# Expert value sums of a PEER layer: from half of each group by Strassen's scheme to all of it

## What is computed

```python
def block(args):
    xb, eb, gb = args
    act = jax.nn.gelu(jnp.einsum('td,tkd->tk', xb, u[eb]))
    return jnp.einsum('tk,tkd->td', gb * act, v[eb])
```

## Time and profile before

| | before |
|---|---|
| median of 3 runs | 1782.0 us (1780.98 to 1785.47) |
| the profiled execution, its time | 1781.31 us |
| its span, first to last instruction | 1779.5 us |
| TensorE busy | 1722.6 us, 97% |
| VectorE busy | 1460.9 us, 82% |
| ScalarE busy | 723.3 us, 41% |
| GpSimd busy | 381.7 us, 21% |

### The profile page before, as it was taken

The page is one execution under the profiler, slowest core; times in us unless marked ns, Lnnn a source line. Parts: engine busy times, 40 slices in busy tenths (PEclk is TensorE's granted clock), DMA queues, the critical chain, the costliest instruction groups (busy, mean ns, idle before and its releaser), DMA issues.

```text
span 1779.5 us, 24820 instructions
## 1 busy us (share of the span) xinstructions
PE 1722.6 (97%) x8316; PEld 1397.7 (79%) x8316; DVE 1460.9 (82%) x2495; ACT 723.3 (41%) x903; POOL 381.7 (21%) x171
## 2 busy tenths in 40 slices
PE   5999999999999999999999999999999999999997
PEld 4774688888777788878888888888888888888885
DVE  7898779999699953388888788887878888787889
ACT  2451433332389962344343343433334343343430
POOL 1000264664300014431111111111111111111102
PEclk8999999999999999999999999999999999999999
DMA  9544210245369997654444444444444444444431
GB/s 382 220 161 165 115 43 1 101 142 191 123 192 284 283 287 257 233 195 149 148 144 148 165 147 159 145 141 150 149 169 147 149 146 147 154 147 166 150 122 70
DMA packets 137358, 293.07 MB, mean 165 GB/s; under 512 B 8256, under 2 KB 73920, under 8 KB 134624
## 3 DMA queue, kind: packets, MB, share of 16 engines
q1 hardware_dynamic: 135600, 287.34, 47.2%
q0 software_dynamic: 1424, 4.85, 0.8%
q10 hardware_dynamic: 288, 0.29, 0.1%
HBM read 237.93 MB, written 54.53 MB: 164 GB/s over the span
## 4 chain that ended last, share of the span: by engine, by line
PE 79%; DVE 13%; issue 3%; ACT 1%; DMA 1%; POOL 1%; DVEq 0%; SPq 0%; ACTq 0%; POOLq 0%
PE bank L1018 25%; PE bank L1020 25%; PE bank L1019 25%; DVE arena L1699 1%; DVE arena L1693 1%; DVE acc L1699 1%; DMA wbuf<-ada_w_dram 1%; DVE acc L1693 1%; PE bank L993 1%; PE bank L1097 1%; DVE arena L1361 1%; DVE u_lo L1686 1%; PE bank L1142 1%; PE bank L1146 1%; DVE u_lo L1908 1%
## 5 line engine op out<-in xcount | busy, mean ns | idle before, releaser
L1018 PE MATMUL bank<-h_hi,u_hi 128*128 128x512 f32 x1272 | 501.4, 394 | 5.7 <-ACT w_raw L872 2.5
L1020 PE MATMUL bank<-h_hi,u_lo 128*128 128x512 f32 x1272 | 495.6, 390 | 0.0
L1019 PE MATMUL bank<-h_lo,u_hi 128*128 128x512 f32 x1272 | 495.0, 389 | 0.0
L1018 PE MATMUL bank<-v_hi,w_hi 128*128 128x512 f32 x932 | 362.5, 389 | 0.0
L625 POOL TENSOR_TENSOR u_lo<-u_raw,u_hi 128x1024 fp32r<-128x1024 f32 x62 | 158.6, 2558 | 784.4 <-ACT u_hi L878 776.2
L1018 PEld LDWEIGHTS bank<-h_hi,u_hi 128*128 128x128 f32 x1272 | 238.8, 188 | 56.6 <-issue 6.8
L1020 PEld LDWEIGHTS bank<-h_hi,u_lo 128*128 128x128 f32 x1272 | 238.7, 188 | 50.8
L1019 PEld LDWEIGHTS bank<-h_lo,u_hi 128*128 128x128 f32 x1272 | 239.0, 188 | 49.0 <-issue 0.7
L1018 PEld LDWEIGHTS bank<-v_hi,w_hi 128*128 128x128 f32 x932 | 174.9, 188 | 36.4
L847 ACT ACTIVATE v_hi<-v_raw 128x1024 fp32r<-128x1024 f32 x124 | 128.2, 1057 | 185.2 <-PE bank L1020 140.0
L1019 PE MATMUL bank<-v_lo_y,w_hi 128*128 128x512 f32 x496 | 192.9, 389 | 0.0
(11 more groups left out here) (243 smaller groups left out, 2532.6 us busy)
## 6 DMA issues: line engine op xcount, KB each, us to landing
u_raw<-ut_dram SPq DMA_DIRECT2D x128, 512.0 KB, 4.0
v_raw<-v_dram SPq DMA_DIRECT2D x128, 512.0 KB, 3.3
gate_in<-gates_dram SPq DMA_DIRECT2D x64, 512.0 KB, 3.2
wbuf<-ada_w_dram SPq DMA_DIRECT2D x10, 2048.0 KB, 14.9
early_dram<-arena SPq DMA_DIRECT2D x64, 256.0 KB, 2.3
gates_dram<-wbuf SPq DMA_DIRECT2D x4, 4096.0 KB, 16.0
w_raw<-early_dram SPq DMA_DIRECT2D x64, 256.0 KB, 2.8
gates_dram<-arena SPq DMA_DIRECT2D x3, 4096.0 KB, 16.0
```

Of the source, the lines that this page charges most:

```text
L1018: pe.matmul(out, a_hi, b_hi, start=(k == 0), stop=False)
L1019: pe.matmul(out, a_hi, b_lo, start=False, stop=False)
L1020: return pe.matmul(out, a_lo, b_hi, start=False, stop=(k == n - 1))
```

## The change

Both pairs of a group go by Strassen's scheme. Each of the seven products takes both pairs into the same bank (two block products, six matmuls), so a group has 28 block products in place of 30, that is 84 matmuls in place of 90, and 11 sums are read by VectorE in place of 13 (`SUMS`). In exchange the sums of blocks are made for both pairs. On VectorE and ScalarE one operation covers the same block of both pairs, so it has twice the columns, as two runs. The operands S2 and T2 share a slot with S3 and T3 and are made after the products of S3 and T3. The second `late_inputs` moves ahead, right behind the products of S3 and T3.

VectorE's operations in a group, by columns of one operation:

| | before | after |
|---|---|---|
| weigh | 4 x 512 | 1 x 1024, 2 x 512 |
| add_up (one input in PSUM) | 13 x 512 | 11 x 512 |
| weight_sums | 4 x 256 | 4 x 512 |
| value_sums | 4 x 512 | 4 x 1024 |
| lo_w | 4 x 512, 1 x 768 | 1 x 512, 3 x 1024 |
| lo_v | 4 x 1024, 1 x 1536 | 1 x 1024, 3 x 2048 |

```diff
-SUMS = 13
+SUMS = 11
-A11, S3, A12, A22, S1, S2, S4, YA11, YA21, YA12, YA22 = range(11)
-B11, T3, B21, B22, T1, T2, T4, YB11, YB12, YB21, YB22 = range(11)
+A11, S3, A12, A22, S1, S4 = range(6)
+B11, T3, B21, B22, T1, T4 = range(6)
+S2, T2 = S3, T3
...
+            def product(b, t, w, v, opens=True, closes=True):
+                for r in range(2):
+                    w_of = tuple(of[:, r, w, t * P:(t + 1) * P] for of in (w_hi, w_lo))
+                    v_of = tuple(of[:, r, v, :] for of in (v_hi, v_lo))
+                    k = r + (0 if opens else 1)
+                    mm = thrice(bank[b][:, :], k, k + (1 if closes and r else 2), (w_of, v_of))
+                return mm
...
                 for t in range(2):
-                    product(4 + t, t, 0, 1, S3, T3).then_inc(s_vmm, 1)
+                    product(4 + t, t, S3, T3).then_inc(s_vmm, 1)
+                late_inputs(i, T_EARLY + 3, 2, BANK_U)
+                pe.wait_ge(s_wlo, i * 4 + 3)
...
-            v_sums, w_sums = (t.rearrange("p a n -> p (a n)") for t in (v_sum, w_sum))
+            v_a, v_b = v_raw[:, 0:4:2, :], v_raw[:, 1:4:2, :]
+            w_a, w_b = w_raw[:, 0:4:2, :], w_raw[:, 1:4:2, :]
+            a11, a21, a12, a22 = w_a[:, :, 0:HALF], w_a[:, :, HALF:], w_b[:, :, 0:HALF], w_b[:, :, HALF:]
+            b11, b12, b21, b22 = v_a[:, :, 0:DH], v_a[:, :, DH:], v_b[:, :, 0:DH], v_b[:, :, DH:]
...
+            def firsts(i):
+                if not isinstance(i, int) or i > 0:
                     ve.wait_ge(s_acc, i * SUMS)
                 add_up(i, 1, acc_p7[:, halves[0]], 4)
                 add_up(i, 2, acc_p7[:, halves[1]], 5)
-                ve.wait_ge(s_wlo, i * 5 + 5)
-                weight_sums(i, 1)
-                ve.wait_ge(s_vlo, i * 5 + 5)
+                lo_w(i, 4, S2, S2 + 1, w_sum2[:, :, :])
+                lo_v(i, 4, T2, T2 + 1, v_sum2[:, :, :])
+            def group(i):
+                weigh_early(i, 1)
+                weigh(i, 1, 1)
+                firsts(i)
+                ve.wait_ge(s_vlo, i * 4 + 4)
                 value_sums(i, 1)
-                lo_w(i, 6, (A11, S3 + 1), w_raw[:, 0, :])
+                weigh(i, 1, 3)
                 add_up(i, 3, acc_p2[:, halves[0]], 6)
                 add_up(i, 4, acc_p2[:, halves[1]], 7)
-                lo_v(i, 6, (B11, T3 + 1), v_raw[:, 0, :])
+                ve.wait_ge(s_wlo, i * 4 + 4)
+                weight_sums(i, 1)
                 add_up(i, 5, acc_p3[:, halves[0]], 4)
                 add_up(i, 6, acc_p3[:, halves[1]], 5)
-                lo_v(i, 7, (B21, B22 + 1), v_raw[:, 1, :])
-                weigh(i, 1, 2)
-                weigh(i, 1, 3)
...
+                lo_v(i, 5, B21, B22 + 1, v_b)
+                add_up(i, 7, acc_p6[:, :], 6)
+                lo_w(i, 5, A11, S3 + 1, w_a)
+                add_up(i, 8, acc_p5[:, halves[0]], 7)
+                add_up(i, 9, acc_p5[:, halves[1]], 4)
+                lo_v(i, 6, B11, T3 + 1, v_a)
+                lo_w(i, 6, S1, S4 + 1, w_14)
                 add_up(i, 10, acc_p4[:, halves[0]], 5)
                 add_up(i, 11, acc_p4[:, halves[1]], 6)
-                lo_w(i, 8, (A12, A22 + 1), w_raw[:, 1, :])
-                add_up(i, 12, acc_y22[:, halves[0]], 7)
-                add_up(i, 13, acc_y22[:, halves[1]], 4)
-                lo_w(i, 9, (YA11, YA21 + 1), w_raw[:, 2, :])
-                lo_w(i, 10, (YA12, YA22 + 1), w_raw[:, 3, :])
-                lo_v(i, 10, (T1, T4 + 1), v_sums)
+                lo_w(i, 7, A12, A22 + 1, w_b)
+                lo_v(i, 7, T1, T4 + 1, v_14)
```

More of the change, by code:

```diff
@@ L160, in build @@
         xt = before.enter_context(nc.sbuf_tensor("xt", [P, TB, D], F32))
+        ramp = before.enter_context(nc.sbuf_tensor("ramp", [P, NG, PAD_P], F32))
+        hsum, hmean = (before.enter_context(nc.sbuf_tensor(n, [P, H, KD], F32)) for n in ("hsum", "hmean"))
         before.close()
@@ L287, in last_w @@
             if m < TAIL:
-                return w_slots(*((A11, S3 + 1), (A12, A22 + 1), (YA11, YA21 + 1), (YA12, YA22 + 1))[m])
+                r, a = m // 2, m % 2 * 2
+                return tuple(t[:, r, a:a + 2, :].rearrange("p s n -> p (s n)") for t in (w_hi, w_lo))
             j = m - TAIL
@@ L893, in _, with seconds @@
-            hi_w((YA11, YA21 + 1), w_raw[:, 2, :])
-            act.wait_ge(s_w, 4)
-            hi_w((YA12, YA22 + 1), w_raw[:, 3, :])
-            def group(i):
-                act.wait_ge(s_wlo, i * 5 + 3)
+            act.wait_ge(s_ws, 2)
+            hi_w(A11, S3 + 1, w_a)
+            act.wait_ge(s_vs, 4)
+            hi_v(T1, T4 + 1, v_14)
+            act.wait_ge(s_ws, 4)
+            hi_w(S1, S4 + 1, w_14)
+            hi_w(A12, A22 + 1, w_b)
+            def seconds(i):
+                act.wait_ge(s_wlo, i * 4 + 3)
@@ L913, in group @@
                 act.wait_ge(s_ws, i * 4 + 8)
                 act.wait_ge(s_vmm, i * SUMS + 9)
-                hi_w((S1, S4 + 1), w_sums)
+                hi_w(S1, S4 + 1, w_14)
                 act.wait_ge(s_vmm, i * SUMS + 11)
-                hi_w((A12, A22 + 1), w_raw[:, 1, :])
-                act.wait_ge(s_vmm, i * SUMS + 13)
-                for j in range(2):
-                    act.wait_ge(s_v[2 + j], i * 16 + 32)
-                    hi_v((YB11 + 2 * j, YB12 + 2 * j + 1), v_raw[:, 2 + j, :])
@@ L1265, in group @@
                 for t in range(2):
                     pe.wait_ge(s_acc, i * SUMS + (1 + t))
-                    product(4 + t, t, 0, 3, S4, B22)
-                    product(4 + t, t, 1, 3, YA11, YB12)
-                    product(4 + t, t, 2, 3, YA12, YB22).then_inc(s_vmm, 1)
-                late_inputs(i, T_EARLY + 3, 2, BANK_U)
-                pe.wait_ge(s_vlo, i * 5 + 5)
-                for t in range(2):
-                    pe.wait_ge(s_acc, i * SUMS + (3 + t))
-                    product(6 + t, t, 0, 1, S1, T1).then_inc(s_vmm, 1)
@@ L1780, in _ @@
             ve.wait_ge(s_x0, 2 * TB)
[L1781 to L1782 removed]
+            ve.memset(acc_p4, 0.0).then_inc(s_zacc, 1)
             partial_modulation(11)
```

364 lines of the change are left out of this document (155 added, 209 removed).

## The result

The changed kernel took a median of 1799.63 us (1796.11 to 1804.29, 4 runs), against 1783.43 us (1780.98 to 1785.47, 4 runs) for the kernel before on the same chip. The ratio is 1.0093, with a 95% interval of 1.0065 to 1.0121: slower by 16 us. The forecast had 1838 us, 55 us slower, and a range from 1814. Direction and bound came out as forecast, the size less than a third of it.

What follows compares the result with a forecast made beforehand. The prediction took VectorE to bound the changed kernel, with both splits paid: 788.7 (ahead of group 0) + 31.95 + 928.2 + 25.4 + 61.9 = 1836.2 us of span, plus 1.8: 1838 us, range 1814 to 1852.

Steps and rivals of the forecast that it cites:

- Its own work of 28.35 us a group: VectorE's operations in a loop group after the change, without the splits, priced start to start: 28.35 us against 24.1 before.
- The exclusion: VectorE operations with both inputs in SBUF and GpSimd's split exclude each other; each split excludes 2.4 us of SBUF work.
- the first split: GpSimd's first low-half subtraction of a group: asks during `lo_v` T14, runs ahead of the joint weighing, costs VectorE 2.4 us.
- GpSimd does not starve: Premise from group 0 before: GpSimd, asking during L1754, runs right after it, though VectorE's L1755 was ready.
- the forecast's 33.15 us: VectorE's time per group after: 28.35 us of work plus 4.8 for two splits, against TensorE's 29.92.
- Groups 1 to 28: Term of the sum along VectorE for the loop groups: 28 x 33.15 = 928.2 us.
- The rest: Terms behind group 28: group 29 without the sums of blocks, 25.4 us, and the end, 61.9 us.
- Its four splits beside four low halves stay: At the end, GpSimd's four splits stay beside VectorE's four low halves; the end takes 61.9 us, 63.0 before.
- Rival 2: One of a group's two splits falls on bank readings: 31.95 us a group, about 1804; chance 0.05.
- the mean near 3.6 us of the joint weighing (L1700): Sign of being right: in the profile after, the joint weighing has a mean near 3.6 us in place of 1.22.
- likely L1741: Sign of being right: one of the sums of V, likely this one, has a mean near 3.6 us, not 1.22.
- splits of GpSimd that lie over bank readings: Sign of being wrong: in the profile after, GpSimd's splits run beside VectorE's readings of banks.

Runs made afterwards that it cites:

- e4: The kernel before with both GpSimd subtractions of a loop group cut to an eighth of their columns, part of the work left out: 1782.14 us, ratio 0.9999.
- e1: The changed kernel with both GpSimd subtractions of a loop group cut to an eighth of their columns, part of the work left out: 1754.33 us, ratio 0.9836.
- e6: The changed kernel, complete, with sums 3 and 4 read ahead of the weighing of product 3: 1769.48 us, ratio 0.9928.
- g2: The changed kernel with one added wait of VectorE for itself, eleven operations ahead of the seam that the first split lost: 1833.59 us.
- e2: The changed kernel with only the first GpSimd subtraction of a loop group cut to an eighth, part of the work left out: 1785.62 us, ratio 1.002.
- e7: The changed kernel with one added wait of VectorE for its own last low half, right at the lost seam before the joint weighing: 1830.66 us, ratio 1.0266.
- the six runs behind it: The changed kernel with one such wait placed 1, 2, 4, 5, 8 or 11 operations ahead of the lost seam: 1831.53, 1830.05, 1833.93, 1830.22, 1836.59, 1833.59 us.
- f1: The changed kernel with one added wait of VectorE for itself, one operation ahead of the seam that the first split lost: 1831.53 us.
- e9: The changed kernel, complete, with the four low halves of h at the end made by VectorE and not GpSimd: 1791.32 us, ratio 1.0043.

## Why the prediction was wrong in size

**What held.** TensorE bounded the groups before, with the splits hidden (e4: no change). VectorE bounds them after, but for the 0.2 us that it waits for a bank. Its own work of 28.35 us a group, summed from rows of before, is borne out: 31.45 less 0.8 and 2.2 for the splits and 0.2 at the reading is 28.25. 2048 columns in two runs take 2.28 us. TensorE alone would need 29.92 (e1). Bank readings are exempt (e6). The exclusion, for a whole operation each, is the rule that the prediction also named from the Trainium skill ("SBUF — State Buffer", "SBUF: two separate sides"): the trace agrees, with 3.41 us for an operation of 1.22 (g2). The time of the first product, 783.9 in the forecast, is 783.2 in e1, whose start is not delayed; TensorE stands 4.54 us for it.

**The step that failed** is the one on the first split: "It gets its turn at that operation's end, in front of the joint weighing. Loss: the whole 2.4 us. Even if it misses that seam, the next two operations have both inputs in SBUF." It missed that seam and the next one, and fell on the two readings: 0.8 us, and 0.4 of the group's time (e2). "GpSimd does not starve" was the premise that failed, and its ground was one case in group 0 of the trace before, L1754 to L1755. There VectorE had just waited for itself (L1754 starts 0.45 us behind L1752, L1755 only 0.34 behind L1754); here it had not for 14 operations. e7 and the six runs behind it bring the hand-over back with one such wait and give the forecast's world: 32.5 to 32.9 us and 1830 to 1837 us, within the range of 1814 to 1852. What is left to the forecast's 33.15 us is its second error, of size: a split that gets the seam costs 2.1 to 2.2 us and not 2.4 (L1700 3.42 - 1.22; L1743 3.30 - 1.22 in f1). The rows don't show why.

**The sum in its own terms.** VectorE's start of group 0 was forecast at 788.7 us and is 795.3 - 6.9 = 788.4. Group 0 took 34.4 us, not 31.95: 28.35, a wait of 1.9 for a load, and both splits paid (L1700 3.23 and L1741 3.41 in place of 1.22). Groups 1 to 28 took 28 x 31.455 = 880.7, not 928.2: 47.5 us less. The rest took 92.1 us, not 87.3: "Its four splits beside four low halves stay" was wrong too, by the same mechanism, though it there moved the cost from VectorE's chain to TensorE's. 788.4 + 6.9 + 34.4 + 880.7 + 92.1 = 1802.5. The forecast of the span, 1836.2, is 33.7 us over this: the 47.5 of the groups, less 13.8 that the other terms gave back, 6.9 of them the late start of this execution.

Where the 16 us are, by the start of each group's first product in the two traces (group 0, 1 and 29: 778.76, 810.04 and 1685.88 us before; 790.34, 826.52 and 1707.33 after): 790.34 - 778.76 - 6.9 = 4.7 us ahead of group 0; 36.2 - 31.3 = 4.9 in group 0; 880.8 - 875.8 = 5.0 in groups 1 to 28; and 95.2 - 93.6 = 1.6 behind. Sum 16.2 (from the spans, 1802.5 - 1779.5 - 6.9 = 16.1). In e9 the last stretch is 87.7 us (1789.5 - 1701.77), so TensorE's stop for the low halves of h and what follows it cost 7.5 of the 95.2. The three first products after, TensorE in order of time:

```profile
790.34 0.79 PE L992 MATMUL bank<-v_hi,w_hi 128*128 128x512 f32 x1 [4.54 <-DVE w_lo L1710]
...
826.52 0.39 PE L992 MATMUL bank<-v_hi,w_hi 128*128 128x512 f32 x1
...
1707.33 0.39 PE L992 MATMUL bank<-v_hi,w_hi 128*128 128x512 f32 x1
```

**The rivals.** Rival 2 is what happened, "One split of the two falls on readings", at 1804 us and with a chance of 0.05. That its time lies so near is in part luck: its group of 31.95 us is 0.5 too long, 14 us over 28 groups, and group 0 and the end gave 7 of them back. Its condition was wrong: no request came 3 us earlier (1.82 us into `lo_v`, forecast 1.6 to 2.1); it was kept waiting. In the forecast a missed seam was written off in half a sentence, and nothing was worked out for missing two. Of the signs, the mean near 3.6 us of the joint weighing (L1700) did not come, it was 1.22 us in the groups. The second split came in behind L1743, two operations further on than "likely L1741" says, so that the weighing L1692 paid. And "splits of GpSimd that lie over bank readings", a sign of being wrong, came for the first split.

## What to carry to other kernels

Where VectorE with two SBUF inputs and GpSimd share the ports, ask for each GpSimd operation which VectorE operation it will meet, and put readings of PSUM there: moving two readings by one place was worth 30 us here. Do not take from one hand-over that the next goes the same way: note whether VectorE has waited for itself shortly ahead, and put both outcomes, with their prices, into the range. A wait that takes 0.1 us can decide that, so after any edit of such a stream look again at where GpSimd's operations come in. And when an engine that follows another becomes the bound, small splits may be cheaper on it (4.6 us here) than beside it (9.5 or 17.7).

## What the runs showed of the hardware

- A waiting GpSimd operation can be passed over at several seams in a row: two in a group of the changed kernel (4.48 us for 2.4 of work), five at its end (7.77 us for the first of the four). It got in at the first reading of a bank (in the group) or where VectorE waited for itself (at the end). A wait of VectorE for itself up to 11 operations ahead changed this in each of seven runs; 14 ahead, and at the end 8 ahead, it did not.
- The reverse is there too: in the kernel before GpSimd's four low halves ran without a gap (9.46 us) while one VectorE operation waited for all of them (one of the four L1908 of the earlier trace rows took 10.33 us). In the changed kernel, from 1758 us on, they took turns one by one, L1882 at 3.3 to 3.4 us each. What tells these two apart I did not find.
- After a stop of 4.56 us TensorE's next matmuls started 0.43 us apart in place of 0.227, until 1775.98, and its granted clock was 0.70 over these 10 us. After its stop of 4.54 us ahead of group 0 it was the same: 0.43 us apart until 796.05, and a granted clock of 0.50 from 790 to 795.
